# Attention stage: VectorE takes the minima of the next unit before it combines the last one; transposes move to two units later, value products to three

## The reference

```python
sc = jnp.einsum('bhcqd,bhckd->bhcqk', qb, kt).astype(jnp.float32) * scale   # c = 0, 1: two score matrices
mask = kpos[None, :] <= qpos[:, None]
sc = jnp.where(mask, sc, -jnp.inf)
p = jax.nn.softmax(sc, axis=-1)
a = p[:, :, 0] - lam * p[:, :, 1]
return jnp.einsum('bhqk,bhkv->bhqv', a.astype(vt.dtype), vt)
```

## Time and profile before

| | |
|---|---|
| device time, median of 3 runs (lowest to highest) | 4649.63 us (4648.69 to 4650.72) |
| the profiled execution's own time, its span | 4649.02 us, 4647.2 us |
| busy over the span: TensorE, VectorE, ScalarE | 97%, 57%, 37% |
| units of attention, first to last row minimum | 3550.7 to 3721.5 us |
| busy in the 177 us from 3550 to 3727: TensorE, VectorE, ScalarE | 159.8, 136.7, 127.0 us |
| first matmul of the next stage | 3747.18 us |

### The profile page before, as it was taken

How to read it: one execution, slowest core, us unless ns; L and a number is a source line. 1 busy time by engine, 2 the same in 40 slices (tenths; PEclk the granted TensorE clock), 3 DMA queues, 4 the chain that set the end, 5 groups by cost and what they waited for, 6 DMA issues and landing times. The chain is left out here.

```text
span 4647.2 us, 66517 instructions
## 1 busy us (share of the span) xinstructions
PE 4526.9 (97%) x27608; PEld 3674.0 (79%) x27608; DVE 2670.9 (57%) x3938; ACT 1728.5 (37%) x2924; POOL 457.6 (10%) x371
## 2 busy tenths in 40 slices
PE   7999999999999999999999799899999989999999
PEld 4888877778999999999999444688777567888887
DVE  3245545555637777777777686546453755555543
ACT  3234443444424544555444333211343742111111
POOL 0000000000002333332335000000010000000000
PEclk8999999999999999999999999999999999999999
DMA  5244344434430110111021352423210021122222
GB/s 210 99 145 150 131 147 141 145 132 150 168 120 15 46 54 33 62 43 59 28 100 47 98 179 86 150 104 118 82 46 19 19 113 64 68 77 73 100 87 95
DMA packets 155978, 441.79 MB, mean 95 GB/s; under 512 B 17168, under 2 KB 47120, under 8 KB 140448
## 3 DMA queue, kind: packets, MB, share of 16 engines
q1 hardware_dynamic: 140624, 383.98, 23.8%
q0 software_dynamic: 9296, 32.58, 2.0%
q10 hardware_dynamic: 5760, 20.97, 1.2%
HBM read 294.86 MB, written 141.56 MB: 94 GB/s over the span
## 5 line engine op out<-in xcount | busy, mean ns | idle before, releaser
L202 PE MATMUL pr_ps<-uhl,w_split 128*128 128x512 f32 (+1 forms) x1520 | 586.1, 386 | 3.1 <-DVE w_split L145 2.2
L206 PE MATMUL pr_ps<-uhl,w_split 128*128 128x512 f32 (+1 forms) x1520 | 571.1, 376 | 0.0
L205 PE MATMUL pr_ps<-uhl,w_split 128*128 128x512 f32 (+1 forms) x1520 | 570.6, 375 | 0.0
L1583 DVE TENSOR_TENSOR b_G<-b_ps,cst 128x512 fp32r<-128x512 f32 x560 | 381.4, 686 | 65.1 <-PE b_ps L1362 61.7
L138 ACT ACTIVATE w_split<-share 128x2048 fp32r<-128x2048 f32 x64 | 122.6, 1915 | 700.8 <-DVE ou_vc L3304 271.1
L202 PEld LDWEIGHTS pr_ps<-uhl,w_split 128*128 128x128 f32 x1520 | 286.7, 189 | 81.5 <-issue 29.2
L205 PEld LDWEIGHTS pr_ps<-uhl,w_split 128*128 128x128 f32 x1520 | 286.9, 189 | 56.1 <-issue 5.8
L206 PEld LDWEIGHTS pr_ps<-uhl,w_split 128*128 128x128 f32 x1520 | 286.6, 189 | 52.6
L1124 POOL TENSOR_SCALAR b_Mr<-b_tri 128x512 fp32r<-128x512 f32 x80 | 117.7, 1489 | 1878.4 <-DVE b_tri L1567 1878.4
L202 PE MATMUL ou_ps<-ou_a,w_split 128*128 128x512 f32 x704 | 277.1, 394 | 7.7 <-DVE ou_a L2160 7.7
L205 PE MATMUL ou_ps<-ou_a,w_split 128*128 128x512 f32 x704 | 275.4, 391 | 0.0
(11 more groups left out here) (498 smaller groups left out, 10082.3 us busy)
## 6 DMA issues: line engine op xcount, KB each, us to landing
w_ring<-in_w_in SPq DMA_DIRECT2D x41, 1024.0 KB, 5.5
proj<-pr_stage SPq DMA_DIRECT2D x160, 256.0 KB, 2.0
share<-in_w_up SPq DMA_DIRECT2D x24, 1024.0 KB, 4.8
ar<-share SPq DMA_DIRECT2D x32, 512.0 KB, 2.8
b_AR<-ar SPq DMA_DIRECT2D x64, 256.0 KB, 2.9
pr_raw<-proj SPq DMA_DIRECT2D x48, 256.5 KB, 3.5
ada<-in_ada_w SPq DMA_DIRECT2D x24, 512.0 KB, 5.6
ff<-ou_vc ACTq DMA_DIRECT2D x24, 512.0 KB, 2.6
```

The source lines that it names most:

```text
L202: mm = nc.tensor.matmul(dst, a[0], b[0], start=start, stop=False)
L205: nc.tensor.matmul(dst, a[0], b[1], start=False, stop=False)
L206: return nc.tensor.matmul(dst, a[1], b[0], start=False, stop=stop)
L1583: L[x]["dve"].done(V.tensor_tensor(Gs[x][m % 2][:], heads(x, 0 if m else 1), rep(K(f"lev{m}"), 4), ALU.mult), f"{n}.G{m}")
```

## The change

VectorE now takes both minima of unit n before it does `soft(n-1)`. TensorE splits the scores in two: `sc(n, 0)`, then `tr(n-2)`, then `sc(n, 1)`, and after the gates `av(n-3)`. ScalarE keeps `turn_out(n-1)` at its place, and takes `take(n-3)`. The reciprocals of the first map's sums are taken once per head in `mean` rather than per unit. Recurrence and normalisation work moves to other values of `t`. ScalarE's activation tables are loaded by name, with a set for `norm` that holds logarithm and exponential. Lines of the new kernel are a few off those of the old.

```diff
@@ TensorE
-                def sc(n):
+                def sc(n, c):
...
                 for n in range(NU):
                     h, t = units[n]
-                    sc(n)
+                    sc(n, 0)
+                    if n >= 2:
+                        tr(n - 2)
+                    sc(n, 1)
                     if t == 1:
                         gates(h, 0)
...
-                    if n >= 1:
-                        tr(n - 1)
-                    if n >= 2:
-                        av(n - 2)
+                    if n >= 3:
+                        av(n - 3)
+                tr(NU - 2)
+                av(NU - 3)
                 tr(NU - 1)
                 av(NU - 2)
@@ ScalarE
                     exp(n, 1)
                     if n >= 1:
                         turn_out(n - 1)
-                    if n >= 2:
-                        take(n - 2)
+                    if n >= 3:
+                        take(n - 3)
                     if t == 0 and h >= 2:
                         end(h - 2)
                     if t == 1:
+                        if h:
+                            nc.scalar.preload_act_table_set("exp_and_others")
                         open_a(h)
-                        if h:
-                            square(h - 1)
                     if t == 2:
                         open_x(h)
                         decay(h)
                     if t == 3:
                         decay2(h)
                         bend(h)
-                    if t == 4 and h:
-                        norm(h - 1)
+                        if h:
+                            square(h - 1)
                     if t == 5:
                         rise(h)
-                A(warm[:], G["eps"][:, 0:1], ACT.Ln)
+                        nc.scalar.preload_act_table_set("natural_log_exp_and_others")
+                        if h:
+                            norm(h - 1)
                 turn_out(NU - 1)
+                take(NU - 3)
                 take(NU - 2)
@@ VectorE
-                    s.done(V.reciprocal(rc[:, b], sm[:, b]))
+                    s.done(V.reciprocal(rc[:, b:b + 1], sm[:, h % 2, t, 1:2]))
                     s.wait()
-                    if t == 0 and h >= 2:
-                        dve.wait_ge(meaned, h - 1)
-                    s.done(V.tensor_copy(r0[:, h % 2, t:t + 1], rc[:, b, 0:1]))
...
                 def mean(h):
                     dve.wait_ge(squared, h + 1)
                     s.done(V.tensor_reduce(ms[:], sq[:], AX.X, ALU.add))
+                    s.done(V.reciprocal(r0[:, h % 2], sm[:, h % 2, :, 0]))
...
+                    peak(n, 0)
+                    peak(n, 1)
                     if n >= 1:
                         soft(n - 1)
-                    peak(n, 0)
-                    peak(n, 1)
...
-                    if t == 2 and h:
-                        mean(h - 1)
+                    if t == 0 and h:
+                        run(h - 1)
+                    if t == 1 and h:
+                        leave(h - 1)
+                    if 1 <= t <= 4 and h + 1 < RT:
+                        tap(h + 1, t - 1)
                     if t == 3:
                         admit(h)
                     if t == 4:
                         spare(h)
-                    if t == 5 and h:
-                        scale(h - 1)
+                        if h:
+                            mean(h - 1)
                     if t == 6:
                         enter(h)
-                    if t == 7:
+                        if h:
+                            scale(h - 1)
+                    if t == 7 and h + 1 == A_HEADS:
                         run(h)
-                    if t == 0 and h:
-                        leave(h - 1)
-                    if t >= 4 and h + 1 < RT:
-                        tap(h + 1, t - 4)
```

More of the change, by code:

```diff
@@ L2589, in attend @@
         p, aT = sb("p", [P, 2, 2, T]), sb("aT", [P, 2, T // P, P])
-        nb, sm, rc = sb("nb", [P, 2, 2]), sb("sm", [P, 2, 2]), sb("rc", [P, 2, 2])
+        nb, sm, rc = sb("nb", [P, 2, 2]), sb("sm", [P, 2, 8, 2]), sb("rc", [P, 2])
         ratio = sb("ratio", [P, 2])
@@ L2617, in attend @@
         TR = ps[:, 4:6].rearrange("p a f -> p (a f)")
-        warm = ctx.enter_context(nc.sbuf_tensor("at_warm", [P, 1], F32))
         flat_at = lambda h, x: ps[:, 4 + x] if h + 1 == A_HEADS else ps[:, 1 + 2 * x]
@@ L2644, in _ @@
                 pe.wait_ge(rounded, 2)
-                def sc(n):
+                def sc(n, c):
                     h, t = units[n]
                     w = (t + 1) * P
-                    if t == 4:
+                    if t == 4 and c == 0:
                         pe.wait_ge(th_x, h + 1)
-                    for c in range(2):
-                        if n >= 1:
[L2653 to L2658, removed]
+                    if n >= 1:
+                        pe.wait_ge(exp_ready, 2 * n - 1 + c)
+                    r = slice(64 * c, 64 * c + 64)
+                    for b in range(0, w, HALF):
+                        nc.tensor.matmul(S[:, c, b:min(w, b + HALF)], qk[r, h, t * P:(t + 1) * P],
+                                         qk[r, 4 + h, b:min(w, b + HALF)], start=True, stop=b + HALF < w)
+                    nc.tensor.matmul(S[:, c, t * P:w], id_r[:], mask_r[:], start=False, stop=True).then_inc(scores, 1)
                 def tr(n):
@@ L2732, in exp @@
                 def exp(n, c):
-                    w = (units[n][1] + 1) * P
+                    h, t = units[n]
+                    w = (t + 1) * P
                     act.wait_ge(nb_ready, 2 * n + c + 1)
+                    if h >= 2 and t == 0 and c == 0:
+                        act.wait_ge(meaned, h - 1)
                     if n >= 2 and c == 0:
@@ L2737, in exp @@
                     A(p[:, n % 2, c, 0:w], S[:, c, 0:w], ACT.Exp, scale=-1.0, bias=nb[:, n % 2, c:c + 1],
-                      accum_out=sm[:, n % 2, c:c + 1]).then_inc(exp_ready, 1)
+                      accum_out=sm[:, h % 2, t, c:c + 1]).then_inc(exp_ready, 1)
                 def turn_out(n):
@@ L2881, in soft @@
                     dve.wait_ge(exp_ready, 2 * n + 2)
-                    s.done(V.reciprocal(rc[:, b], sm[:, b]))
+                    s.done(V.reciprocal(rc[:, b:b + 1], sm[:, h % 2, t, 1:2]))
                     s.wait()
-                    if t == 0 and h >= 2:
-                        dve.wait_ge(meaned, h - 1)
-                    s.done(V.tensor_copy(r0[:, h % 2, t:t + 1], rc[:, b, 0:1]))
-                    s.done(V.scalar_tensor_tensor(ratio[:, b:b + 1], sm[:, b, 0:1], lam[:, 3:4], rc[:, b, 1:2], ALU.mult, ALU.mult))
+                    s.done(V.scalar_tensor_tensor(ratio[:, b:b + 1], sm[:, h % 2, t, 0:1], lam[:, 3:4], rc[:, b:b + 1], ALU.mult, ALU.mult))
                     s.wait()
```

## The result

The changed kernel takes 4742.12 us (median of 4 runs, 4739.90 to 4742.97) against 4650.18 for before beside it: ratio 1.0197, 95% interval 1.0179 to 1.0214, 92 us slower. The forecast was 4694 (4667 to 4718). The direction and the place were right.

The account below looks back on a forecast made before the run. Only the attention stage, some 177 us, could change; TensorE's idle and clock losses there were put at 20 us. Forecast: 4649.6 + 28 for waits + 16 for clock = 4694 us, range 4667 to 4718.

Parts of the forecast that it names:

- Where ScalarE stands: In-order ScalarE waits at turn_out(n-1) for tr(n-1), with its extra work X(n) and exp(n+1, 0) queued behind.
- The waits, 28 us: Attention stage: net time added by TensorE's stalls at full clock, 28 us, giving 4678.
- The single stops: TensorE stalls in us: second gate 2.2; scores t = 4 2.3, t = 5 3.0, t = 7 3.5; t = 6 transposes 1.1; first gate 1.8.
- 48 lost and 20 recovered: Attention stage: new stalls sum to 48.3 us over four heads; the old order's idle and clock losses recovered are 20.
- 15 x 1.7 = 25 us; I take two thirds, 16: TensorE's clock: fifteen stalls of 2.1 us or more, each dropping it; upper end 25 us, 16 taken.
- the 1.7 us: TensorE: matmul time lost per clock fall after a long stop, read from four-microsecond windows near 0.6.
- A slow second map fills part of the next stall instead and may avert the next drop.: TensorE's second score map: run at low clock, it fills stall time; a reason for 16 us of clock, not 25.
- Rival 4: Every stall drops TensorE's clock, and VectorE's later extras delay the minimum of t = 5: 4715 and above, chance 0.12.
- VectorE's later extras ahead of t = 5: VectorE's moved extra work, 3.8 us at t = 4, adds to the minimum of t = 5.
- The price of the Trainium skill: ScalarE table loads: 1.38 us drain, 2.66 us per switch, would add some 15 us; the sum left it out.

Follow-up runs that it names:

- e2: Changed kernel with score matmuls contracting over all 128 rows instead of 64 (another output): 4682.17 us, ratio 1.0068 to the kernel before.
- e12: Changed kernel with ScalarE's copy of the transposes one unit later and scores over 128 rows (another output): 4649.83 us, ratio 1.0002 to the kernel before.
- e1: Changed kernel with ScalarE's copy of the transposes one unit later, turn_out(n-2) instead of turn_out(n-1): 4708.46 us, ratio 1.0127 to the kernel before.
- e10: Changed kernel with extra unread fp32 matmuls over 128 rows placed where TensorE stops: 4687.75 us, ratio 1.0073 to the kernel before.
- e11: Kernel before with score matmuls contracting over all 128 rows instead of 64 (another output): 4643.90 us, ratio 0.9984 to the kernel before.
- e3: Changed kernel with extra unread matmuls over 128 rows, most of them one iteration ahead of the stops meant: 4738.18 us, ratio 1.0188 to the kernel before.
- e9: Kernel before with only the change's ScalarE activation tables and the moves of norm and scale: 4652.68 us, ratio 1.0007 to the kernel before.
- e5: Kernel before with two activation table loads added once, in head 1 at t = 3, so TensorE stops once: 4654.82 us, ratio 1.0012 to the kernel before.
- e8: Kernel before with the value products av(n-2) moved between the two score maps: 4655.44 us, ratio 1.0005 to the kernel before.

## Why the prediction was wrong, step by step

- **Where ScalarE stands.** Right. `turn_out(n-1)` waits for `tr(n-1)` in every unit (117.7 us in 32), with X(n) and the exponential behind it. Taking that wait away gives back 32 us in the kernels where the clock recovers (e2 to e12), and 34 where it does not (after to e1); both figures hold some clock.
- **The waits, 28 us.** Right within what was measured: 34, 26 to 42, at full clock (e10). The single stops: second gate 2.02 and scores of t = 4 2.10 (2.2 and 2.3 forecast), t = 5 and t = 7 2.50 and 3.66 in e2 (3.0 and 3.5), t = 6's transposes 0.99 in e10 (1.1), the first gate of head 2 1.60 in after (1.8). The split of the net into 48 lost and 20 recovered did not hold: with the copy out of the way e12 should then have been 20 us below e11 and is 6 above, with 25.2 us of stops left. The copy's place is worth 32 us at most, not 48, and nothing of the 20 came back in these two kernels; the two errors cancel in the net. That the net of 28 lies so near 34 is in part luck.
- **The clock, "15 x 1.7 = 25 us; I take two thirds, 16".** This is the step that failed. Between after and e10 lie 54 us by the medians and 58 by the ratios to before (1.0197 and 1.0073); between after and e2 lie 60, with the form of the matmuls in them. So 54 to 58 where 16 was taken and the upper bound was 25. The mis-sized factor is the 1.7 us, the price of one fall. It came from the earlier trace rows, where the clock was back after four microseconds. But what stands behind those two stops in the earlier trace rows is eight transposes, over 128 rows, followed by value products. What was forecast to stand behind the new stops is scores over 64 rows, and there no row of before shows a fall at all. An upper bound would have had to let a fall last to the end of the head: in after it lasted 40 us.
- **"A slow second map fills part of the next stall instead and may avert the next drop."** The first half is right (0.93 and 0.67 instead of 3.0 and 3.5), and it was read the wrong way round: the clock had not come back, so there was no next drop to avert. A short stop in a profile is then no sign of a small loss.
- **Rival 4** (every stall drops the clock, 4715 and above, 0.12) held the result (4742), by part of its mechanism: not more falls, but falls that last. Its other half, VectorE's later extras ahead of t = 5, shows no sign in the stops: 2.50 in e2 and 2.70 in e3 where 3.0 was forecast without them.
- **The price of the Trainium skill** (ScalarE: Activation LUTs, What ACT_TABLE_LOAD costs: 2.66 us for each switch of table) would have added some 15 us, an estimate from that page. After, e9 and before all show 1.28 and the next activation 1.29 or 1.30 after the start; by the trace that rule is not at work here.

What stays open: why the clock comes back under 128-row products and not under 64-row ones in a busy TensorE (e2, e3 and e5 show that it does, not by what rule). The edit of e2 changes two things at once: the rows of the scores, and the change of form between scores and mask, behind which the mask starts 0.5 us sooner (1.42 us after the scores in e11, 1.91 before); no run took these apart. Open too is what share of after's waits each of the moved pieces of VectorE's work has, which no run took apart.

## What to carry to other kernels

Price a stall by the instructions that stand behind it, not only by its length: here a stop of 2 us cost 1.7 us of clock ahead of 128-row transposes, and ahead of 64-row scores it was followed by half clock for most of a head. A recovery read at one place is no bound for another place. When a change moves an in-order engine's producer later, move the consumer on every engine by the same step; the copy left behind cost some 32 us, its share of the clock included, and with it moved the deeper order was still only level (e12). If engines wait for TensorE while TensorE shows no idle time, look at the granted clock and at the length of equal matmuls before looking for a longer path.

## What the runs showed of the hardware

- TensorE's clock stayed at 1.2 GHz through three windows of 5 us in which it was busy 5.00 of 5.00 with matmuls mostly over 64 rows (after, 3650 to 3665), and returned in the midst of a group of 128-row products in e3 (granted clock 0.56 from 3651.2 to 3653.2, then 1.00). The Trainium skill (TensorE: Matmul & The Clock Gate, Part 1: The HAM clock gate) has the full clock come back once the array has been busy for a while, and that part says nothing of rows. By the busy time that the profile shows this trace does not agree, and the measurement decides.
- Stops of 1.24 us (e1) and 0.93 us (e8, at 3583.74) ahead of 64-row scores were followed by half clock. Stops of 1.43 and 1.63 us ahead of 128-row scores were not (e12, at 3586.92 and 3619.34), nor was one of 1.90 ahead of value products (e8, at 3594.50). In e12 one of 1.90 ahead of transposes (at 3594.75) and one of 2.06 ahead of scores (at 3625.54) were, and each fall was over within the two windows shown:

```profile
3594.00:3598.00 4.00, 3.25 (x20) 3.28 (x21) 2.24 (x7) 2.50 (x7) 0.00 (x0) 0.73 0.00 0
3598.00:3602.00 4.00, 4.00 (x21) 3.17 (x20) 3.52 (x8) 1.46 (x6) 0.00 (x0) 0.85 0.01 2
...
3624.00:3628.00 4.00, 2.46 (x6) 1.38 (x7) 2.50 (x5) 3.49 (x7) 0.00 (x0) 0.82 0.00 0
3628.00:3632.00 4.00, 4.00 (x19) 2.89 (x17) 1.90 (x2) 3.93 (x6) 0.00 (x0) 0.76 0.00 0
```

- Scores over 128 rows cost TensorE less than the same columns over 64 rows between products over 128 rows: 139.4 us busy in the stage against 157.4 (e11, before), of which the kernel keeps 5.
- Work without a purpose made the kernel faster: 21 extra products per head (13 in head 0), near 10 us of TensorE time a head at 0.45 us each, took 54 us off after (e10). It stays 34 us behind before, so it is a probe and no remedy; none of the versions with the right output beats the kernel before.
